# The decay recurrence of one core's kernel: levels up to 64 tokens in 64x64 blocks, a compact merge buffer, and another order of the linear work beside it

## What is computed

```python
def _chunk_scan(q, logf, k, v):
    ...
        bcum = jnp.cumsum(lfc, axis=2)
        o_inter = jnp.einsum("bgtk,bgkv->bgtv", qc * jnp.exp(bcum), state)
        diff = bcum[:, :, :, None, :] - bcum[:, :, None, :, :]
        decay = jnp.exp(jnp.where(causal[:, :, None], diff, -jnp.inf))
        scores = jnp.einsum("bgtk,bgtsk,bgsk->bgts", qc, decay, kc)
        o = o_inter + jnp.einsum("bgts,bgsv->bgtv", scores, vc)
    ...
def hgrn2_mixer(h, w_in, lb, gn_g, w_out):
    q, z_f, z_b, v, g = jnp.split(h @ w_in, 5, axis=-1)
    ...
    logf = jnp.logaddexp(jnp.log(lb_h), jnp.log1p(-lb_h) + jax.nn.log_sigmoid(z2))
    k2 = (1 - lb_h) * jax.nn.sigmoid(-z2)
    out = _chunk_scan(q2, logf, k2, v2)          # both directions, 8 heads of 128
    o = out[:, :, 0] + out[:, ::-1, 1]
    ... # norm of each head, gain, times silu(g)
    return o @ w_out
```

## Time and profile before

| | us |
|---|---|
| median of 3 runs (lowest, highest) | 2355.43 (2354.51, 2355.98) |
| the profiled execution's own time | 2356.45 |
| its span, first to last instruction | 2354.8 |
| PE busy | 2190.1 (93%) |
| DVE busy | 1285.4 (55%) |
| ACT busy | 837.6 (36%) |
| recurrence, from the first "diag" to the last norm's sum | 1566.5 to 1940.8 |

### The profile page before, as it was taken

One profiled execution on the slowest core, in us unless ns is written; L12 is line 12 of the kernel. 1 busy time (PEld: TensorE's weight loads), 2 busy tenths in 40 slices (PEclk: granted clock), 3 DMA queues, 4 the chain that ended last, 5 costly groups with the idle time before them and its releaser, 6 DMA issues.

```text
span 2354.8 us, 26024 instructions
## 1 busy us (share of the span) xinstructions
PE 2190.1 (93%) x10364; PEld 1731.2 (74%) x10364; DVE 1285.4 (55%) x1900; ACT 837.6 (36%) x1313; POOL 181.8 (8%) x153
## 2 busy tenths in 40 slices
PE   6999898898999999896999999998898889999998
PEld 5776786576888886563688888877777667888886
DVE  4455656436466666797464343366557664443443
ACT  4343544335222232312442232254444453332331
POOL 2230104022000002110100000100000001000001
PEclk9999999999999999997999999999999999999999
DMA  5212331024666663344222323121111122323221
GB/s 163 72 55 90 108 105 63 30 72 143 216 228 232 236 220 111 86 129 128 72 90 90 108 90 103 60 79 54 46 46 54 45 81 72 107 90 107 90 95 49
DMA packets 214073, 242.02 MB, mean 103 GB/s; under 512 B 6465, under 2 KB 200385, under 8 KB 207809
## 3 DMA queue, kind: packets, MB, share of 16 engines
q1 hardware_dynamic: 213376, 238.26, 31.3%
q10 hardware_dynamic: 576, 2.10, 0.2%
HBM read 229.39 MB, written 2.10 MB: 98 GB/s over the span
## 4 chain that ended last, share of the span: by engine, by line
PE 75%; DVE 10%; ACT 6%; issue 3%; SPq 3%; DMA 2%; POOL 1%; DVEq 0%; POOLq 0%; ACTq 0%
PE bank L998 20%; PE bank L999 19%; PE bank L1000 19%; SPq L1990 3%; DVE wL L1518 3%; PE bank L1019 2%; PE bank L1020 2%; PE bank L1021 2%; PE bank L1159 2%; PE bank L1182 1%; PE bank L1114 1%; PE bank L1069 1%; DVE hX L1830 1%; DVE aacc L1686 1%; PE bank L1062 1%
## 5 line engine op out<-in xcount | busy, mean ns | idle before, releaser
L998 PE MATMUL bank<-hH,wH 128*128 128x512 f32 (+1 forms) x1672 | 668.6, 400 | 40.6 <-DVE hL L1524 16.3
L999 PE MATMUL bank<-hL,wH 128*128 128x512 f32 (+1 forms) x1672 | 652.6, 390 | 0.0
L1000 PE MATMUL bank<-hH,wL 128*128 128x512 f32 (+1 forms) x1672 | 652.2, 390 | 0.0
L1518 DVE TENSOR_TENSOR wL<-raw,wH 128x1024 fp32r<-128x1024 f32 (+1 forms) x378 | 412.2, 1132 | 218.9 <-ACT wH L1218 218.6
L1218 ACT ACTIVATE wH<-raw 128x1024 fp32r<-128x1024 f32 (+1 forms) x378 | 335.6, 937 | 412.9 <-PE bank L1000 302.9
L998 PEld LDWEIGHTS bank<-hH,wH 128*128 128x128 f32 x1672 | 320.0, 191 | 131.2 <-issue 51.7
L1000 PEld LDWEIGHTS bank<-hH,wL 128*128 128x128 f32 x1672 | 318.9, 191 | 65.7
L999 PEld LDWEIGHTS bank<-hL,wH 128*128 128x128 f32 x1672 | 319.9, 191 | 62.4 <-issue 2.4
L998 PE MATMUL bank<-hidH,wH 128*128 128x512 f32 x768 | 304.3, 396 | 6.7 <-DVE hidL L1666 6.7
L999 PE MATMUL bank<-hidL,wH 128*128 128x512 f32 x768 | 303.0, 395 | 0.0
L1000 PE MATMUL bank<-hidH,wL 128*128 128x512 f32 x768 | 302.6, 394 | 0.0
(11 more groups left out here) (198 smaller groups left out, 2166.3 us busy)
## 6 DMA issues: line engine op xcount, KB each, us to landing
raw<-in_mlp SPq DMA_DIRECT2D x64, 1024.0 KB, 5.3
araw<-in_ada_w SPq DMA_DIRECT2D x48, 1024.0 KB, 4.9
raw<-in_w_ff SPq DMA_DIRECT2D x32, 1024.0 KB, 7.3
raw<-in_hgrn_in SPq DMA_DIRECT2D x32, 512.0 KB, 3.7
raw<-in_w_in SPq DMA_DIRECT2D x12, 1024.0 KB, 5.2
u<-uc SPq DMA_DIRECT2D x128, 67.5 KB, 2.1
raw<-in_conv_in SPq DMA_DIRECT2D x16, 512.0 KB, 4.2
raw<-in_w_mv SPq DMA_DIRECT2D x4, 1024.0 KB, 6.3
```

The source lines that it names most:

```text
L998: mm(out, wh[:, k, m:m + 128], xh[:, k, 0:width], start=k == 0, stop=False)
L999: mm(out, wh[:, k, m:m + 128], xl[:, k, 0:width], start=False, stop=False)
L1000: i = mm(out, wl[:, k, m:m + 128], xh[:, k, 0:width], start=False, stop=k == KB - 1)
L1518: e.tensor_tensor(wL[:, s, c], raw[:, r, c], wH[:, s, c].bitcast(F), SUB).then_inc(*s_wlo.up(n, x))
```

## The change

Levels 1 to 64, and the products of the tokens with themselves, are computed in blocks of 64x64: each of the four diagonal blocks gives two, and the two write PSUM partitions 0 to 63 and 64 to 127, so that they use the two halves of TensorE's columns. Levels 1 to 32 are merged under the mask in a buffer hC of 128x256 instead of in hS, and a new ACT item "spread" copies hC to hS (two copies on 64 partitions each) after the merge of level 32. Level 64 is copied to hS by ACT like level 128 ("off", no mask). Each level is one step; level 256, the output and the norm are three more: 11 steps. Linear work stands behind every step, at size/11 units a step, none ahead of the first step; the order of it is changed (next head's projections first, values at heads 0, 2, 4, gates at heads 1, 3, 5, 6 and four at 7). At the end the outputs of heads 0 to 6 are split before head 7's level 128, and the first three double units of the output projection stand between head 7's last steps.

```diff
...
-            for lev in range(9):
-                g = 1 << lev
-                if 0 < lev <= 6:
-                    yield
+            for lev in range(8):
                 b, free = self.lin.get()
-                if g <= 64:
-                    do("level", h=h, lev=lev, s=keys, b=b, after=free)
+                do("level", h=h, lev=lev, b=b, s=keys, after=free)
+                if lev < 6:
                     self.tmps.put(keys, ("mm", "level", h, lev))
-                elif g == 128:
-                    do("level7", h=h, b=b, after=free)
-                    self.lin.put(b, ("act", "off7", h, 1))
-                else:
-                    do("level8", h=h, half=0, b=b, after=free)
-                    self.lin.put(b, ("act", "off8", h, 0))
-                    b, free = self.lin.get()
-                    do("level8", h=h, half=1, b=b, after=free)
-                    self.lin.put(b, ("act", "off8", h, 1))
-                if g < 256:
-                    do("decayed", h=h, lev=lev)
-                    if g < 64:
-                        s, free = self.tmps.get()
-                        do("gather", h=h, g=2 * g, s=s, after=free)
-                        keys = s
-                    do("decays", h=h, lev=lev)
-                if g <= 64:
+                do("decay_keys", h=h, lev=lev)
+                if lev < 5:
+                    keys, free = self.tmps.get()
+                    do("gather", h=h, g=2 << lev, s=keys, after=free)
+                if lev < 6:
                     do("put", h=h, lev=lev, b=b)
                     self.lin.put(b, ("dve", "put", h, lev))
+                else:
+                    do("off", h=h, lev=lev, b=b, sfree=sfree[x])
+                    self.lin.put(b, ("act", "off", h, lev, 1))
+                if lev == 5:
+                    do("spread", h=h, sfree=sfree[x])
                 yield
+            for up in range(2):
+                b, free = self.lin.get()
+                do("level8", h=h, half=up, b=b, after=free)
+                self.lin.put(b, ("act", "off8", h, up))
...
+            yield
             o, ofree = self.obk.get()
             do("hout", h=h, o=o, after=ofree)
...
             do("hsq", h=h, o=o, s=s, b=b, after=(*free, *free2))
-            yield
             do("hnorm", h=h, o=o, s=s, b=b)
...
+            yield
...
-        gates_at = {4: (0,), 5: (1,), 6: (2,), 7: (3, 4, 5, 6, 7)}
-
-        def beside(h):
-            if 0 < h < 4:
-                yield from self.linear_tm(("hv", h), "hgrn_in", 0, 3072 + 256 * h, 256, src, to_hv)
+        values_at = {0: 1, 2: 2, 4: 3}
+        gates_at = {1: (0,), 3: (1,), 5: (2,), 6: (3,), 7: (4, 5, 6, 7)}
+
+        def beside_scan(h):
+            if h + 1 < KB:
+                yield from project(h + 1)
+            if h in values_at:
+                yield from self.linear_tm(("hv", values_at[h]), "hgrn_in", 0, 3072 + 256 * values_at[h], 256, src, to_hv)
...
-            if h + 1 < KB:
-                yield from project(h + 1)
 
         self.fresh_tm("hv0", "hgrn_in", 0, 3072, src, to_hv)
         run(project(0))
-        for h in range(KB):
-            steps = (8 if 0 < h < 4 else 0) + 4 * len(gates_at.get(h, ())) + (12 if h < KB - 1 else 0)
-            run(weave(beside(h), scan(h), RH / (steps - 3), start=-2 * RH / steps))
+        for h in range(KB - 1):
+            size = 12 + (8 if h in values_at else 4 * len(gates_at[h]))
+            alongside(scan(h), beside_scan(h), size / 11)
+        last = scan(KB - 1)
+        alongside((next(last) for _ in range(7)), beside_scan(KB - 1), 16 / 6.5)
+
+
+        def split(j):
+            do("ho_split", j=j, after=(("mm", *self.piece_done[last_h]),))
+
+        last_h = len(self.pieces) - 1
+        for j in range(KB - 1):
+            split(j)
+        out = self.linear("hgrn_out", "hgrn_out", 0, 0, 1024, ("h", "ho"), self.to_x("r1x", (1, 2), "m1x", True), fresh=True)
+        for _ in range(3):
+            next(last)
+            next(out)
+        run(last)
         gate_out(KB - 1)
-        last_h = self.pieces and len(self.pieces) - 1
-        for j in range(KB):
-            do("ho_split", j=j, after=(("mm", *self.piece_done[last_h]),))
-        run(self.linear("hgrn_out", "hgrn_out", 0, 0, 1024, ("h", "ho"), self.to_x("r1x", (1, 2), "m1x", True), fresh=True))
+        split(KB - 1)
+        run(out)
...
                     for i in range(4):
-                        c = slice(128 * i, 128 * i + 128)
-                        m = mm(banks[it["b"]][:, c], tmp[:, it["sk"], c], tmp[:, it["sq"], c], start=True, stop=True)
+                        for c in range(2):
+                            t = slice(128 * i + 64 * c, 128 * i + 64 * c + 64)
+                            m = mm(banks[it["b"]][64 * c:64 * c + 64, 64 * i:64 * i + 64], tmp[:, it["sk"], t],
+                                   tmp[:, it["sq"], t], start=i == 0, stop=True, skip_group_check=True)
                     m.then_inc(*s_mm.up("diag", h))
...
+                    if lev < 7:
                         for i in range(4):
-                            c = slice(128 * i, 128 * i + 128)
-                            m = mm(banks[it["b"]][:, c].rearrange("p (n u j) -> p n u j", u=2, j=g), tmp[:, it["s"], c],
-                                   half(h, g, 2, 128 * i, 128), start=True, stop=True)
-                        m.then_inc(*s_mm.up("level", h, lev))
-                    elif kind == "level7":
+                            for c in range(2):
+                                t, other = 128 * i + 64 * c, 128 * i + 64 - 64 * c
+                                out = banks[it["b"]][64 * c:64 * c + 64, 64 * i:64 * i + 64]
+                                if lev < 6:
+                                    out = out.rearrange("p (n u j) -> p n u j", u=2, j=g)
+                                    keys, asks = tmp[:, it["s"], t:t + 64], half(h, g, 2, t, 64)
+                                else:
+                                    keys, asks = hX[:, x, c, t:t + 64], hX[:, x, 3 - c, other:other + 64]
+                                m = mm(out, keys, asks, start=i == 0, stop=True, skip_group_check=True)
...
-                    pe.wait_ge(*s_dve.at("put", h, 6))
+                    pe.wait_ge(*s_act.at("spread", h, 1))
...
+                    do(hC[:, h % 2, :], banks[it["b"]][:, 0:256], ACT.Copy).then_inc(*s_act.up("put", h))
...
+                elif kind == "spread":
+                    h = it["h"]
                     x = h % 2
...
+                    act.wait_ge(*s_dve.at("put", h, 5))
+                    for c in range(2):
+                        do(view(hS, 2048 * x + 64 * c, [[640, 4], [1, 64]], 64 * c, 64),
+                           hC[64 * c:64 * c + 64, x, :].rearrange("p (i t) -> p i t", i=4), ACT.Copy).then_inc(
+                            *s_act.up("spread", h, c))
+                elif kind == "off":
...
+                    for c in range(2):
+                        if lev == 6:
+                            dst = view(hS, 2048 * x + 64 - 64 * c, [[640, 4], [1, 64]], 64 * c, 64)
+                            got = bank[64 * c:64 * c + 64, 0:256].rearrange("p (i t) -> p i t", i=4)
+                        else:
+                            dst = view(hS, 2048 * x + (512 if c else 128), [[1024 + 256, 2], [1, 128]])
+                            got = bank[:].rearrange("p (n u t) -> p n u t", n=2, u=2)[:, :, c, :]
+                        do(dst, got, ACT.Copy).then_inc(*s_act.up("off", h, lev, c))
...
-                    dg = bass.AP(tensor=hS[:].tensor, offset=2048 * (h % 2), ap=[hS[:].ap[0], [640, 4], [1, 128]])
-                    mk = bass.AP(tensor=msk[:].tensor, offset=128 * (lev + 1), ap=[msk[:].ap[0], [0, 4], [1, 128]])
-                    e.copy_predicated(dg, mk, banks[it["b"]][:].rearrange("p (i t) -> p i t", i=4)).then_inc(
+                    e.copy_predicated(hC[:, h % 2, :].rearrange("p (i t) -> p i t", i=4),
+                                      view(msk, 64 * lev, [[0, 4], [1, 64]]),
+                                      banks[it["b"]][:, 0:256].rearrange("p (i t) -> p i t", i=4)).then_inc(```

The number of linear matmuls is unchanged. With it the queues change as follows. On ACT in the middle of a head whose next head's first gate z is due (before: head 4; lines as above: L1450 gather, L1439 and L1440 sigmoids, L1218 high parts, L1467 level 128):

```order
L1450 ACTIVATE tmp<-hX 128x512 [waits s_dve_tile] x3
L1202 ACT_TABLE_LOAD
L1439 ACTIVATE hX<-bank 128x512 [waits s_psum_ready]
L1440 ACTIVATE hT<-bank 128x512
L1218 ACTIVATE wH<-raw 128x512 [waits s_raw_landed1]
L1218 ACTIVATE wH<-raw 128x512
L1467 ACTIVATE hS<-bank 128x2x128 [waits s_psum_ready]
L1467 ACTIVATE hS<-bank 128x2x128
```

More of the change, by code:

```diff
@@ L23 @@
 BUSY = 4
[L24 removed]
+RW, RM = 1.4, 0.44
 VEC = {}
@@ L741, in scan @@
             sk, sq = head.pop(h)
-            s, free = self.tmps.get()
-            do("gather", h=h, g=1, s=s, after=free)
-            keys = s
+            keys, free = self.tmps.get()
```

(34 more changed lines are left out.)

50 lines of the change are left out of this document (19 added, 31 removed).

## The result

| | before | changed |
|---|---|---|
| median of 20 runs each (us) | 2352.31 | 2361.74 |
| lowest to highest | 2349.46 to 2359.91 | 2355.53 to 2365.48 |
| ratio, 95% interval | | 1.0035 [1.0027, 1.0043] |
| the profiled execution | 2356.45 | 2360.15 |

The kernel became slower by 0.35%, 8.2 us by the ratio (6 to 10 by its interval; the medians lie 9.4 apart); the prediction was 3.9 us faster (2351.5) with 0.24 on slower.

The account below looks back on a forecast made before the run. TensorE's own queue order, losing waits and half clock, was the bound. Start 5.5 + 47.3 + 2 x 45.6 + 3 x 47.0 + 45.7 + 46.75 = 377.5 against 381.4, 3.9 less: median 2351.5 us, range 2334 to 2370.

Parts of the forecast that it names:

- A group of 64x64 costs 0.73: Level's eight 64-column products: 0.44 plus 0.2 way out and 0.09 way in, 0.08 us below the old 0.81.
- Start 5.5: Ahead of the first "diag": 3.3 us wait for the sum of keys, 1.6 half clock, 0.6 first group.
- Odd heads: Heads 1, 3, 5 with gates: 35.3 us work plus 11.6 waits and clock, 47.0 each, against 44.7 for heads 4 to 6.
- the walk: Head-by-head estimate of work, waits and clock through the recurrence in the new order: 377.5 us, against 381.4 before.
- Head 6: Second-last head: no table load ahead of its next silu, so 45.7 us.
- Head 7: Last head: 56.3 us, or 46.75 without 9.55 of moved projection matmuls, against 50.3; 4.0 of it for the clock.
- Even heads 45.6: Heads with values: 41.1 us work plus listed waits, 45.6 against 49.7 before; head 0 takes 47.3.
- chain of level 32 to 128: Odd heads: merge, spread, then table load end xb at 9.5 us against 5.8 of TensorE work: 3.8 wait.
- ScalarE's queue is not as late as walked: Rival, chance 0.22: waits at level 128 and head starts shrink, no half clock follows; 14 us less, 2337.
- The rival on the clock: Chance 0.18: half clock also follows the shorter waits of 1.6 to 2.3 us; 10 us more, 2361.
- No drain: Rival, chance 0.05: changing TensorE's tiling mode costs nothing, a group takes 0.44; 15 us less, 2337.
- halves don't overlap: Rival, chance 0.10: products on TensorE's two column halves run one by one, a group takes 1.17; 21 us more, 2372.

Follow-up runs that it names:

- order alone: Kernel before with only the changed kernel's order of linear work, steps and end, keeping the 128x128 products and no spread: 1.0080 of the kernel before.
- spread later: Changed kernel with spread's two copies behind those of level 64 instead of ahead: 0.9959 of the kernel before.
- the form alone: Kernel before with only the 64x64 blocks, hC, spread and level 64 by ScalarE, in the old order with the old end: 1.0005 of the kernel before.

## Why the prediction was wrong

By its own steps:

- *A group of 64x64 costs 0.73*: 0.61 to the next linear matmul and 0.09 for the way in (0.32 from the last linear matmul to the group, where two linear ones are 0.23 apart), 0.70. Right, and so is the gain in products: 0.10 in each of six groups and 0.7 where "diag" and level 1 stand together, 1.3 a head. That form and order together have just 10.6 us over order alone is in part luck: it is this gain, 6.6 of waits against it, and less half clock. That halves overlap was right too.
- *Start 5.5*: the wait is 3.13 for 3.3. Right, but the half clock behind it lasts 6.8 us and loses 3.4, for 1.6.
- *Odd heads*: 3.86 ahead of level 128 for 3.8, 1.52 ahead of level 32 for 1.65 (the walk named this one, and two in even heads, one level too low), 2.09 at the next head's first level for 2.3 (all from the changed kernel's timeline of TensorE); end of the projection 3.0 for 3.2. Right. Head 6 was priced 1.3 lower because no table load should stand ahead of the silu behind its norm; the load stands there (ScalarE, 1900.25), and the wait is 2.09 as after the others. Head 7 was charged 4.0 for the clock, and lost nothing up to the projection and 1.7 behind it.
- *Even heads 45.6*: this is the step that failed. The walk listed 1.8, 1.2, 0.5, 0.7 and small waits, and had nothing between the output products and the norm's sum; its text gives no reason for that. I took the two halves of a value block there, 2.9 us of work, as cover for square and table load, where the second half's copy stands ahead of both. Pairs of an odd and an even head, 92.6 by the walk, are 96.5 (1616.04 to 1712.50) and 97.3 (1712.50 to 1809.76). The wait that it left out cost 2.6 us beyond TensorE's pace (the wait of 2.48 and 0.16 of the modelled tail ahead of it) in each of three heads and 1.7 of half clock behind two of them, 11.3 by this count, and taking it away gave 9.4. The prediction had named a half clock in even heads as a sign of being wrong: heads 0, 2 and 4 have four such stretches, behind 2.96 ahead of level 16 in head 0, behind the norm's sum in heads 2 and 4, and behind a 2.09 in head 4.

Over the recurrence, 1561.2 (1564.36 - 3.13) to the projection's matmul at 1955.34, less the 9.55 of moved work, and 1.7 for the clock behind, is 386.3 for 377.5, and 4.9 more than the 381.4 of before, where 3.9 less were forecast. The 1940.8 at which both the table of before and the prediction put the last norm's sum is the projection's first matmul, behind the wait of 3.6; the sum stands at 1936.05. Since the walk's head 7 ends at the projection too, like is compared with like. What stands ahead of the recurrence differs by 1 us in favour of the changed kernel.

The walk's chain of level 32 to 128 was right in size, and its reading was still short: it compared 3.8 with the 2.6 of before, and so priced spread at 1.3. What spread stands in the way of was the form's own gift, a last copy of keys one level earlier, 2.9 us a wait and the clock. I didn't see it because a removed operation was costed only by its own time. The rival *ScalarE's queue is not as late as walked* didn't happen: two copies of spread took 0.86, for 0.8, and the wait ahead of level 128 was 3.86. The kernel with spread later comes near its number (0.9959, for 2337 or 0.994), for a reason that it did not name. The rival on the clock happened in part: one of the four like waits of 2.09 was followed by a half-clock stretch. *No drain* and *halves don't overlap* didn't happen.

## What to carry to other kernels

When an order of work is changed by steps, list for every step of the bounding engine what stands ahead of its supplier in the supplier's own queue, and whose result that item waits for: a copy whose matmuls are yet to come makes a cover into a wait. When a change takes an instruction off a side engine, ask which item can move up into its place, and whether a new item is put exactly there; here one line moved by one level was worth 1.3% in the old order. And count units between steps by where their results' copies land, since taking one away moves all that follow.

## What the runs showed of the hardware

The same wait is not always followed by the half clock. In the changed kernel TensorE waits 2.09 us ahead of level 1 in heads 2 and 4 alike (timelines, one head a fence), and the stretches of the two units behind it differ:

```profile
1664.09 0.89 PE L1178 MATMUL bank<-hX,tmp 128*64 128x64 f32 x16 [2.09 <-ACT tmp L1469]
```

```profile
1759.71 0.88 PE L1178 MATMUL bank<-hX,tmp 128*64 128x64 f32 x16 [2.09 <-ACT tmp L1469]
```

```profile
1664.90:1667.85 2.95, 2.95 (x14) 2.18 (x12) 2.63 (x3) 1.41 (x3) 0.00 (x0) 1.00 0.00 0
1760.52:1765.06 4.54, 4.54 (x14) 3.27 (x13) 4.22 (x6) 1.74 (x3) 0.00 (x0) 0.62 0.02 5
1612.14:1616.04 3.90, 3.90 (x27) 3.29 (x27) 0.75 (x1) 1.32 (x2) 0.00 (x0) 1.00 0.02 4
1804.37:1809.76 5.39, 5.39 (x27) 4.78 (x27) 0.75 (x1) 1.32 (x2) 0.00 (x0) 0.68 0.00 0
```

The last two rows are the work behind the wait of 2.47 ahead of the norm's sum in heads 0 and 4: 2.4 GHz in the one, 1.2 in most of the other. So a price of 1.7 us per such wait is a mean at best. What decides it stays open: no run here varied it alone.

Executions of one kernel spread over 10 us (2349.5 to 2359.9 before), and in the traces the first products of the recurrence, behind nearly the same work, start at 1566.51 before and at 1559.78 in the form alone. Most of that is there within the first 100 us of the program, which no edit touches: TensorE's 400th matmul starts at 96.3 in the one trace and at 91.6 in the other, and the mean granted clock of the first 97 us is 0.95 and 1.00.
